# Wide up steps at both ends of the channel mixer, and the low part of a step's second tile made behind the tile

## The reference

```
h  = rmsnorm(x, ffn_norm_g)
up = causal_dwconv(h @ w_ffn_up, ffn_dw_w, ffn_dw_b)     # 1024 -> 2 x 2816, width 3
gt, val = split(up)
x  = x + (silu(gt) * val) @ w_ffn_down                   # 2816 -> 1024
```

## Time and profile before

| | us |
|---|---|
| median of three runs | 809.72 (809.47 to 810.03) |
| the profiled execution | 809.75 |
| its span, first to last instruction | 807.9 |
| TensorE busy | 795.4 (98% of the span) |
| VectorE busy | 623.6 (77%) |
| ScalarE busy | 536.6 (66%) |
| GpSimd busy | 455.2 (56%) |
| granted clock of TensorE, mean | 0.999 |

### The profile page before, as it was taken

How to read it: one execution, slowest core, us unless ns; L and a number is a source line. 1 busy time by engine, 2 the same in 40 slices (tenths; PEclk the granted TensorE clock), 3 DMA queues, 4 the chain that set the end, 5 groups by cost and what they waited for, 6 DMA issues and landing times.

```text
span 807.9 us, 15118 instructions
## 1 busy us (share of the span) xinstructions
PE 795.4 (98%) x6042; PEld 748.7 (93%) x6042; DVE 623.6 (77%) x1181; ACT 536.6 (66%) x890; POOL 455.2 (56%) x139
## 2 busy tenths in 40 slices
PE   8999999999999999999999999999999999999996
PEld 8999989899999999999999999989999988888895
DVE  5899999673458888887779999885434777887885
ACT  6858978773666665656676577887446565656664
POOL 6999678778722223322389987787786023222240
PEclk9999999999999999999999999999999999999999
DMA  8655434445445545555455544434555445555441
GB/s 301 234 190 196 157 113 150 157 164 197 162 169 196 191 174 183 189 203 203 163 183 184 197 159 167 150 113 157 180 212 183 164 176 198 180 198 206 157 157 52
DMA packets 21381, 142.69 MB, mean 177 GB/s; under 512 B 2496, under 2 KB 3008, under 8 KB 4672
## 3 DMA queue, kind: packets, MB, share of 16 engines
q1 hardware_dynamic: 20736, 140.69, 49.4%
q10 hardware_dynamic: 576, 1.04, 0.4%
HBM read 140.68 MB, written 1.05 MB: 175 GB/s over the span
## 4 chain that ended last, share of the span: by engine, by line
PE 87%; DVE 7%; ACT 3%; DMA 1%; issue 1%; SPq 0%; DVEq 0%; ACTq 0%
PE four L1084 16%; PE four L1086 15%; PE four L1085 15%; PE four L1343 15%; PE four L1349 8%; DVE pc L780 3%; PE ps L1084 1%; PE ps L1085 1%; PE ps L1086 1%; PE ps L1372 1%; PE ps L1373 1%; PE ps L1374 1%; PE four L1218 1%; DVE ol L1015 1%; DMA x<-in_x_t 1%; PE ps L1196 1%
## 5 line engine op out<-in xcount | busy, mean ns | idle before, releaser
L267 POOL TENSOR_TENSOR wlo<-raw,whi 128x2048 fp32r<-128x2048 f32 x86 | 397.5, 4627 | 326.0 <-ACT whi L326 315.7
L326 ACT ACTIVATE whi<-raw 128x2048 fp32r<-128x2048 f32 x129 | 245.9, 1906 | 9.6 <-PE four L1086 9.6
L1084 PE MATMUL four<-hh,whi 128*128 128x256 f32 x704 | 201.4, 286 | 0.0
L1086 PE MATMUL four<-hh,wlo 128*128 128x256 f32 x704 | 199.2, 283 | 0.0
L1085 PE MATMUL four<-hl,whi 128*128 128x256 f32 x704 | 199.1, 283 | 0.0
L780 DVE SCALAR_TENSOR_TENSOR pc<-upad,par_all,pc 128x256 f32<-128x256 f32 x404 | 162.8, 481 | 0.1
L1084 PEld LDWEIGHTS four<-hh,whi 128*128 128x128 f32 x704 | 134.9, 192 | 5.2 <-issue 5.2
L1085 PEld LDWEIGHTS four<-hl,whi 128*128 128x128 f32 x704 | 135.0, 192 | 0.0
L1086 PEld LDWEIGHTS four<-hh,wlo 128*128 128x128 f32 x704 | 135.0, 192 | 0.0
L1343 PE MATMUL four<-u_both,whi 128*128 128x512 f32 x512 | 128.0, 392 | 0.0
L1343 PEld LDWEIGHTS four<-u_both,whi 128*128 128x128 f32 x512 | 92.6, 189 | 16.9
(11 more groups left out here) (240 smaller groups left out, 1367.5 us busy)
## 6 DMA issues: line engine op xcount, KB each, us to landing
raw<-in_weights SPq DMA_DIRECT2D x130, 1024.0 KB, 4.8
raw<-in_weights SPq DMA_DIRECT2D x3, 512.0 KB, 7.8
out_y<-qk SPq DMA_DIRECT2D x3, 256.0 KB, 2.4
x<-in_x_t SPq DMA_DIRECT2D x2, 256.0 KB, 4.0
raw<-in_weights SPq DMA_DIRECT2D x2, 256.0 KB, 3.8
x<-in_x_t SPq DMA_DIRECT2D x1, 512.0 KB, 7.0
gate<-in_final_g ACTq DMA_DIRECT2D x1, 512.0 KB, 4.0
out_y<-qk ACTq DMA_DIRECT2D x1, 256.0 KB, 2.9
```

The source lines that it names most:

```text
L267: nc.gpsimd.tensor_tensor(wlo[s][:, :], raw[s][:, :], whi[s][:, :].bitcast(f32), ALU.subtract).then_inc(lo_ready[s], 1)
L326: A(whi[s][:, :], raw[s][:, :], ACT.Copy).then_inc(hi_ready[s], 1)
L1084: MM(out, whi[s][:, w], hi, start=start, stop=False, skip_group_check=accumulate)
L1086: return MM(out, wlo[s][:, w], hi, start=False, stop=stop, skip_group_check=accumulate)
```

## The change

Steps 1 and 10 of each layer get the wide form too, on TensorE, ScalarE and VectorE, all of which ask `BESIDE`. And VectorE makes the low part of a step's second tile directly behind that tile's product, ahead of the split of slot 0; only step 1 still makes, at the old place, the low part of the tile that step 0 has left. The call behind the last step goes, since step 10 makes its own.

```diff
-BESIDE = range(2, FFN_STEPS - 1)
+BESIDE = range(1, FFN_STEPS)
...
                     scale_up(2, 0, l * USES + j + 11, beside(l, j, 0))
-                    hidden_low(k - 1, 1, 1 - parity)
+                    if j == 1:
+                        hidden_low(k - 1, 1, 1 - parity)
                     hidden_tile(k, 0, col, col + FT * 4)
                     split_low(2, j + 11)
                     scale_up(0, 1, l * USES + j + 12, beside(l, j, 1))
                     hidden_low(k, 0, parity)
                     hidden_tile(k + 1, 1, col + 4, col + FT * 4 + 4)
+                    hidden_low(k + 1, 1, parity)
                     if not last:
                         split_low(0, j + 12)
...
                 ffn_step(FFN_STEPS - 1, 0, True)
-                hidden_low(k0 + FT - 1, 1, 0)
```

## The result

The changed kernel takes **821.5 us** (median of four runs, 819.58 to 821.58), the kernel before 809.8 in the same comparison (809.47 to 810.03): ratio 1.014, 95% interval 1.0125 to 1.0155. It is slower, 0.9 us from the forecast of 822.4. The profiled execution took 821.58 us, its span 819.8.

The account below looks back on a forecast made before the run. A loop over VectorE, ScalarE and GpSimd was taken as the bound: per layer +1.92, eight turns at +0.46 (+3.68) and +0.73 give +6.33, so 12.7 on 809.75 makes 822.4 us; range 817 to 825.5.

Parts of the forecast that it names:

- The bound: Channel mixer: a loop over VectorE, ScalarE and GpSimd ends both layers; TensorE's 1.4 us saving is lost in its waits.
- The sums in step 1 and step 10: VectorE's added sums for converted tiles: 1.46 us in step 1 and 0.73 in step 10, per layer.
- L1015 gone, L1007 held in its place: VectorE behind GpSimd's split: the low part leaves, the step's first L1007 is held instead; -0.33 us a turn.
- "I take the reverse likewise, +0.79": GpSimd's split start, while VectorE still splits slot 0: held for that split's whole rest, 0.76 to 0.84 us later.
- its waits of 0.3 in each step: TensorE ahead of the down unit, every step of either layer: waits some 0.3 us for GpSimd's low part.
- The clock: TensorE's longer idle time at layer 0's end drops the clock to 1.2 GHz: some 2 us more, 824.4; chance 0.05.
- GpSimd not held (810.2): GpSimd's split starts regardless of VectorE's slot 0 split; turn 16.40 us, TensorE leads, +0.5, 810.2 us; chance 0.12.
- TensorE as the bound (808.4): Whole mixer: sums and moved part are hidden, only TensorE's 1.4 us saving stays, 808.4 us; chance 0.06.
- TensorE's early arrival in step 2: Layer 0, second unit of step 2: TensorE reaches its low part 1.3 us before VectorE's split has made it.
- the gap at the end of layer 0: TensorE's idle time at layer 0's end grows from 1.0 to some 4 us.

Follow-up runs that it names:

- third experiment: Changed kernel with the second tile's low part behind the split of slot 0 instead of ahead of it: 812.03 us, ratio 1.0028.
- fifth experiment: Changed kernel with GpSimd splitting only 256 of the 2048 columns of slot 1 in the channel mixer: 812.35 us, one run.
- eighth: Kernel before, low part behind slot 0's split, step 10's slot 2 split quartered (last quarter behind last low part), step 10 wide: 813.73 us.
- first, undisturbed: Kernel before with only the wide form in steps 1 and 10 added: 816.14 us; its profiled execution, without a clock fall, 814.22.

## Why the prediction was right, and where it was not

**The bound.** Right. TensorE has 1.4 us less to do and nothing of it shows; the loop over VectorE, ScalarE and GpSimd sets both ends. Both halves of the change lengthen that loop (+4.5 and +4.4 alone), and the third and fifth experiments hand the turn back to TensorE when GpSimd's hold, or most of its split, is taken away.

**The sums in step 1 and step 10**, 1.46 + 0.73 a layer: right, 4.4 expected of the wide form alone and 4.47 measured.

**L1015 gone, L1007 held in its place**: right in kind. The long one is the first L1007 of each step, and its group ends 1.46 us behind GpSimd where it ended 1.85 behind before, so -0.39 and not -0.33. A held instruction ended 0.28 us behind GpSimd both times, the L1015 of 0.42 us (258.40) and the L1007 of 0.48 (260.52); the difference of 0.06 is between their own lengths.

**"I take the reverse likewise, +0.79"** is the step that was mis-sized. The hold is real in this order too, which was the open question. But it is 0.63 us, below the lower end of 0.76 that I had set for a held GpSimd, because I took it to last until L939's recorded end, and it is 0.15 us shorter than that. The rows had a hint: the held L1015 went on at 257.99, as I read it myself, 0.13 before the recorded end of GpSimd's split at 258.12. I used that edge for the term -0.33 and not for the reverse, where it would have given some 0.66. With the 0.06 above, a turn costs 0.24 and not 0.46, and as 18 turns pay it, the loops lost 8.7 us and not 12.7. The first L1011 behind the hold was late by 1.73 (forecast 1.92), the last L1015 of layer 0 by 4.37 (forecast 6.33). The turn became 16.97. That is only 0.04 longer than TensorE's step in layer 0, so its waits of 0.3 in each step are not there in layer 0; in layer 1, 0.36 longer than its step, they are. The Trainium skill, SBUF — State Buffer, section "Who interferes with whom", says that an instruction of VectorE with two SBUF inputs and one of GpSimd that reads SBUF shut each other out and that the order of issue decides which one waits. The runs now agree for both orders, except that by the records the hold is 0.15 us shorter than the overlap.

**The clock.** I gave it 0.05, once, as a rival of +2 us. It fell twice and cost 1.5 and 1.6 us. The price was about right and the chance far too low: the only grounds for 0.05 were that no row of before shows a fall, and no row of before shows a gap that long either.

So the time came within 0.9 us because two errors cancelled: 4.0 too much for the loop, 3.1 missing for the clock. The verdict does not hang on either: the loops alone give 818.6.

**The rivals.** GpSimd not held (810.2): ruled out by the 5.26 us splits. Its picture of what TensorE does then came near: the third experiment, with next to no hold but with L939 in its old place, took 811.07 undisturbed. TensorE as the bound (808.4): ruled out. Of the smaller steps, TensorE's early arrival in step 2 was 1.1 us (forecast 1.3), and the gap at the end of layer 0 3.7 (forecast some 4).

## What to carry to other kernels

In a loop that passes through VectorE and GpSimd, look at which instruction of VectorE with two inputs from SBUF is at work at the moment GpSimd becomes ready, before moving anything there: a 0.42 us instruction put ahead of a long split costs through the split that it pushes under GpSimd's start, and put behind it costs nothing here (808.0 against 809.8, with the form of steps 1 and 10 as before). A hold that falls on one instruction is not gone when that instruction moves; look for the next one of its kind in the queue. And price a wait of TensorE with the clock: here, of eight gaps of 2.4 to 3.7 us at the end of a layer in the profiled executions, four were followed by a fall of the clock, and each fall that was measured cost another 1.5 us or so.

## What was not expected of the hardware

- A held instruction's record begins when it would have started, and the hold is drawn as its length: GpSimd 5.26 us for a 4.63 us split. The waits view shows nothing of it; the max of a line against its median does.
- The hold is shorter than the overlap of the two records: by 0.15 us where GpSimd was second (overlaps of 0.77 and 0.20 us gave 0.62 and 0.05). Where VectorE was second, the held L1015 had only 0.28 us left behind GpSimd's recorded end, of 0.42. Whether the held engine goes on early or has done its own start by then is not shown.
- The granted clock fell behind gaps of TensorE of 3.68 and 2.77 us in the changed kernel, 2.45 in the fifth experiment and 2.68 in the eighth (layer 0). It did not fall behind gaps of 2.45 (third, undisturbed), 2.70 and 2.78 (first, undisturbed) and 3.07 (eighth, layer 1). None of 1.9 us or less at the end of a layer was followed by a fall in a profiled execution. Why the same length does both was not found.
